# A second block with resident weights at one expert position, and an order table for the expert loads

## The reference

```python
def hierarchical_moe(x, wg, bg, we, be, w_gate, w_up, w_down):
    g_prob = softmax(xt @ wg + bg)            # 4 groups, the best one is taken
    e_top_l, e_idx = top_k(logits_of_the_8_experts_of_that_group, 2)
    gates = softmax(e_top_l) * g_top_p
    # each token goes to its 2 experts:
    hb = silu(xb @ w_gate[e]) * (xb @ w_up[e])      # 1024 -> 512
    y  = hb @ w_down[e]                             # 512 -> 1024, summed with the gates
```

## Time and profile before

| What | Value |
|---|---|
| Runs | 1364.5, 1366.34, 1366.96 us |
| Profiled execution: time / span | 1365.07 us / 1363.3 us |
| Mean granted TensorE clock | 0.876 |
| Busy share PE / DVE / ACT / POOL | 78% / 34% / 18% / 1% |
| Mean DMA rate over the span | 343 GB/s, 468.15 MB moved |
| Expert stage of layer 0, first streamed load issued / last down matrix landed | 163.57 us / 597.91 us |
| Expert stage of layer 1, the same | 898.37 us / 1347.15 us |

### The profile page before, as it was taken

The page is one execution under the profiler, slowest core; times in us unless marked ns, Lnnn a source line. Parts: engine busy times, 40 slices in busy tenths (PEclk is TensorE's granted clock), DMA queues, the critical chain, the costliest instruction groups (busy, mean ns, idle before and its releaser), DMA issues.

```text
span 1363.3 us, 21323 instructions
## 1 busy us (share of the span) xinstructions
PE 1069.8 (78%) x9301; PEld 717.3 (53%) x9301; DVE 464.2 (34%) x1167; ACT 244.5 (18%) x557; POOL 6.9 (1%) x28
## 2 busy tenths in 40 slices
PE   8999786856767686789999999887776585676775
PEld 7888543523434243447888888644434252343442
DVE  2351452222222122235655555463222222222123
ACT  2220111111111111123433333211111111111102
POOL 1000000000000000000000000000000000000000
PEclk9999888878877787889999999989788787887789
DMA  9754499999999999984566663469999999999995
GB/s 347 225 224 179 191 428 426 428 426 426 428 426 427 427 428 424 427 303 132 193 216 235 234 226 118 191 273 427 426 427 427 428 425 428 428 425 427 428 401 229
DMA packets 87941, 468.15 MB, mean 343 GB/s; under 512 B 16940, under 2 KB 56104, under 8 KB 62888
## 3 DMA queue, kind: packets, MB, share of 16 engines
q1 hardware_dynamic: 87344, 466.11, 84.2%
q10 hardware_dynamic: 504, 0.67, 0.2%
HBM read 465.68 MB, written 1.08 MB: 342 GB/s over the span
## 4 chain that ended last, share of the span: by engine, by line
PE 39%; issue 36%; DMA 22%; DVE 2%; SPq 1%; ACT 1%; POOL 0%; DVEq 0%; POOLq 0%
DMA w_gu<-in_expert_w_up 18%; PE pb L1192 10%; PE pa L1192 7%; PE acc L1216 4%; DMA w_x<-in_expert_w_up 3%; PE pa L1430 3%; PE wa L1430 2%; PE wb L1439 2%; PE acc L1318 2%; PE pb L1421 2%; PE pb L1247 1%; DMA w_dn<-in_expert_w_down 1%; PE pb L1408 1%; PE wa L1199 1%; PE wb L1619 1%
## 5 line engine op out<-in xcount | busy, mean ns | idle before, releaser
L1430 PE MATMUL pa<-w_gu,arena 128*32 128x256 f32 x1536 | 125.8, 499 | 81.5 <-DMA w_gu<-in_expert_w_up 81.5
L971 DVE TENSOR_SCALAR arena<-arena 128x128 f32<-128x128 f32 x64 | 14.5, 227 | 469.6 <-ACT arena L453 469.6
L1430 PE MATMUL wa<-w_gu,arena 128*32 128x256 f32 x1344 | 98.8, 459 | 64.0 <-DMA w_gu<-in_expert_w_up 62.4
L1430 PEld LDWEIGHTS pa<-w_gu,arena 128*32 128x32 f32 x1536 | 59.4, 142 | 153.0 <-DMA w_gu<-in_expert_w_up 93.7
L453 ACT ACTIVATE arena<-wb 32x256 f32<-32x256 f32 (+1 forms) x263 | 99.1, 377 | 134.7 <-PE wb L1439 122.7
L1192 PE MATMUL pb<-hnT,w_x 128*128 128x256 f32 x496 | 109.9, 380 | 2.4 <-DVE arena L1031 2.4
L1430 PEld LDWEIGHTS wa<-w_gu,arena 128*32 128x32 f32 x1344 | 48.6, 132 | 113.9 <-DMA w_gu<-in_expert_w_up 71.4
L1421 PE MATMUL pb<-arena,hs 128*128 128x128 f32 x480 | 79.5, 334 | 31.5 <-issue 15.1
L1192 PEld LDWEIGHTS pb<-hnT,w_x 128*128 128x128 f32 x496 | 93.4, 190 | 15.0 <-issue 2.8
L1421 PEld LDWEIGHTS pb<-arena,hs 128*128 128x128 f32 x480 | 73.2, 241 | 45.8 <-issue 41.4
L1439 PE MATMUL wb<-w_dn,arena 128*32 128x256 f32 x1440 | 89.2, 391 | 7.7 <-DMA w_dn<-in_expert_w_down 5.0
(11 more groups left out here) (285 smaller groups left out, 1196.1 us busy)
## 6 DMA issues: line engine op xcount, KB each, us to landing
w_dn<-in_expert_w_down SPq DMA_DIRECT2D x45, 2048.0 KB, 26.5
w_gu<-in_expert_w_gate SPq DMA_DIRECT2D x45, 2048.0 KB, 31.6
w_gu<-in_expert_w_up SPq DMA_DIRECT2D x45, 2048.0 KB, 36.0
arena<-in_expert_w_down SPq DMA_DIRECT2D x20, 2048.0 KB, 27.4
w_x<-in_expert_w_gate SPq DMA_DIRECT2D x20, 2048.0 KB, 31.2
w_x<-in_expert_w_up SPq DMA_DIRECT2D x20, 2048.0 KB, 35.7
w_x<-in_odd_in_proj SPq DMA_DIRECT2D x16, 1024.0 KB, 5.4
w_x<-in_odd_in_proj SPq DMA_DIRECT2D x16, 512.0 KB, 5.5
```

The source lines that it names most:

```text
L971: link(v.tensor_scalar(eg, eg, 1.0, None, ALU.add))
L1430: ins = mm(gu[32 * j:32 * j + 32, :, :], xb[:, k, c0:c0 + CAP], w_gu[s][:, :, k, P * j:P * j + P], start=(k == 0), stop=(k == KC - 1))
```

## The change

- `SLOT` is `e % 3` throughout, so the last four experts have the slots 1, 2, 0, 1.
- Position 15 (`WIDE`) has 64 slots. After its first 32 and the combine of its quad, all engines always run `second_block` on the weights that still lie in slot 0. This is in both layers, however many tokens there are.
- `swap_columns` on VectorE exchanges, in the routing tables, the first overfull expert with a number of at least 4 (`PRE`) and expert 15, and writes which expert stands at which position to `order`. SyncE reads each expert's number from `order` from position 4 on.
- The overflow loop is moved behind the second block, from position 27 to 15, and its loads use slot 0. SyncE asks for it before the load of position 18. Expert 15's first 64 tokens don't count as overflow.
- The token counts are taken in TensorE's `route`. `positions`, the copy `PG`, the first `rows_of` and `zero_acc` are moved from position 0 to position 1.
- Some semaphores are merged. The reserve columns of `pos` and their memset go.

The core of the diff:

```diff
-OV_AT = 28
-OV_SLOT = 1
-SLOT = [e % 3 for e in range(OV_AT)] + [2, 0, 1, 0]
+SLOT = [e % 3 for e in range(NE)]
+PRE = 4
+WIDE = 15
+OV_SLOT = SLOT[WIDE]
...
-            def expert_part(l, e, part, after=None):
+            def expert_part(l, e, part, after=None, which=None):
                 s = SLOT[e]
                 if after is not None:
                     sp_.wait_ge(S["dn_done" if part == 2 else "gu_done"], after + 1)
+                    if after % NE == WIDE:
+                        sp_.wait_ge(S["w_dn" if part == 2 else "w_gu"], after // NE + 1)
...
             def overflow_weights(l):
                 sp_.wait_ge(S["table_done"], l + 1)
-                sp_.wait_ge(S["gu_done"], NE * l + previous(OV_AT + 2) + 1)
-                sp_.wait_ge(S["dn_done"], NE * l + previous(OV_AT + 2) + 1)
+                sp_.wait_ge(S["w_dn"], l + 1)
                 k0 = sp_.value_load(table[0:1, l:l + 1], min_val=0, max_val=OV_LIST)
                 k1 = sp_.value_load(table[0:1, l + 1:l + 2], min_val=0, max_val=OV_LIST)
                 with sp_.If(k0 < k1):
...
+            def expert_at(l, e):
+                if e < PRE:
+                    return None
+                return sp_.value_load(order[0:1, NE * l + e:NE * l + e + 1], min_val=0, max_val=NE - 1)
+
             def expert_stream(l):
-                for e in range(3, NE):
-                    if e == OV_AT:
-                        overflow_weights(l)
-                    if e == OV_AT + 2:
+                for e in range(3, NE - 2):
+                    if e == PRE:
+                        sp_.wait_ge(S["order_done"], l + 1)
+                    which = expert_at(l, e)
+                    if e == WIDE + 3:
+                        overflow_weights(l)
                         k1 = sp_.value_load(table[0:1, l + 1:l + 2], min_val=0, max_val=OV_LIST)
                         sp_.wait_ge(S["ov_done"], k1 + 1)
...
+            def swap_columns(l):                      # VectorE, behind gathered(0, l, 1)
...
+                dve.wait_ge(S["cnt_done"], l + 1)
+                link(v.tensor_copy(cnt, wb[:, 0:NE]))
...                                                    # 8 small ones: prefer
+                link(v.tensor_reduce(out=most, in_=prefer, axis=AX, op=ALU.max))
+                link(v.tensor_scalar(other, prefer, most, None, ALU.is_equal))
...                                                    # 3 small ones: here, keep
+                link(v.tensor_tensor(cols2, cols, over(other), ALU.mult))
+                link(v.tensor_reduce(out=at_other[:, 0:6], in_=cols2, axis=AX, op=ALU.add))
...                                                    # 5 more over 6 x 32 columns
+                v.tensor_copy(order[0:1, NE * l:NE * l + NE], ids[0:1, :]).then_inc(S["order_done"], 1)
...
+            def second_block(l):                      # TensorE
+                pe.wait_ge(S["w_vec"], 3 * l + 1)
+                mm(o_B[:, :], o_sel, PG, start=True, stop=True)
+                for c in range(KC):
+                    for t in range(TT):
+                        ins = mm(o_XG[:, c, :], hs[:, t, c, :], o_S[:, t, :], start=(t == 0), stop=(t == TT - 1))
+                ins.then_inc(S["w_b"], 1)
+                pe.wait_ge(S["w_vec"], 3 * l + 2)
+                gate_up(o_xs, 0, SLOT[WIDE], GU[0]).then_inc(S["w_gu"], 1)
+                pe.wait_ge(S["w_vec"], 3 * l + 3)
+                down(o_hT, SLOT[WIDE]).then_inc(S["w_dn"], 1)
+                pe.wait_ge(S["w_act"], 2 * l + 2)
+                combine(l, o_G4, o_y).then_inc(S["w_done"], 1)
...
-                positions(l)
                 for e in range(NE):
...
-                    if e == 0:
+                    if e == 1:
+                        positions(l)
                         pe.wait_ge(S["pg_done"], l + 1)
-                    rows_of(e, l)
-                    if e == 0:
+                        rows_of(0, l)
                         zero_acc()
...
-                    if e == OV_AT - 1:
+                    if e == WIDE:
                         down_of(l, e)
                         combine_of(l, q)
                         pe.wait_ge(S["xs_done"], 2 * (NE // QUAD * l + q + 1) + 2)
+                        second_block(l)
```

More of the change, by code:

```diff
@@ L81 @@
 prep_sel quad_sel b_done g4_done gath_done xs_done gu_done gexp h_done ht_done dn_done y_copied comb_part
-ov_in ov_sel ov_b ov_x ov_gu ov_exp ov_ht ov_dn ov_yc ov_done
+order_done w_vec w_act w_b w_gu w_dn w_done
+ov_in ov_vec ov_act ov_b ov_gu ov_dn ov_done
 """.split()
@@ L148, in trunk_program @@
         ov_tot = sb("ov_tot", [P, 1])
-        ARENA = 11520
+        order = sb("order", [1, 2 * NE], I32)
+        slot_id2 = sb("slot_id2", [P, 1])
+        ARENA = 11392
         arena = sb("arena", [P, ARENA])
@@ L201, in trunk_program @@
         Rs = take(SEQ, rows=NG + NE + 1)
-        pos = take(TT, NE + QUAD)
-        gates = take(TT, NE)
+        cols = take(6, NE)
+        pos, gates, cnt, ids = cols[:, 0:TT, :], cols[:, TT:2 * TT, :], cols[:, 4, :], cols[:, 5, :]
+        other, here, keep, wide = (take(NE) for _ in range(4))
+        prefer, at_other, most = take(NE), take(8), take(1)
         mask = take(TT, NE)
         lg = take(TT, NG + NE)
-        rt1, rt2, oh1, oh2 = (take(TT, NE) for _ in range(4))
+        rts = take(4 * TT, NE)
+        rt1, rt2, oh1, oh2 = (rts[:, TT * i:TT * i + TT, :] for i in range(4))
+        cols2 = rts[:, 0:6, :]
         m8 = take(8, TT)
         dd, ee = take(TT, 8), take(TT, 8)
-        cnt = take(2 * NE + 8)
+        ov_more = take(NE)
         PG = take(2 * SEQ, rows=NE)
@@ L308, in overflow_weights @@
                         sp_.wait_ge(S["ov_done"], k + 1)
-                        e = sp_.value_load(table[0:1, ds(k + 3, 1)], min_val=0, max_val=NE - 1)
+                        p = sp_.value_load(table[0:1, ds(k + 3, 1)], min_val=0, max_val=NE - 1)
+                        e = sp_.value_load(order[0:1, ds(p + NE * l, 1)], min_val=0, max_val=NE - 1)
                         for part in range(2):
@@ L377, in _ @@
             expert_stream(0)
-            sp_.wait_ge(S["gu_done"], OV_AT + 1)
+            sp_.wait_ge(S["gu_done"], NE - 2)
             for c in (2, 1, 0):
@@ L932, in every_fourth, with second_select, second_block @@
                 return a.rearrange("p (m j) -> p j m", j=FF // P)
+            def second_select(l):
+                if l:
+                    dve.wait_ge(S["w_done"], l)
+                link(v.tensor_scalar(o_iota, iota1[:, :], float(CAP), None, ALU.add))
+                v.tensor_scalar(o_sel, ident[0:NE, WIDE:WIDE + 1].to_broadcast([NE, P]), 1.0, None, ALU.mult)
+                v.tensor_tensor(o_S, o_iota.unsqueeze(1).to_broadcast([P, TT, CAP]),
+                                pos[:, :, WIDE:WIDE + 1].to_broadcast([P, TT, CAP]), ALU.is_equal
+                                ).then_inc(S["w_vec"], 1)
+            def second_block(l):
+                dve.wait_ge(S["w_b"], l + 1)
+                link(v.tensor_scalar(o_G4, o_B[:, 0:SEQ], slot_id2[:, :], None, ALU.is_equal))
+                v.tensor_tensor(o_G4, o_G4, o_B[:, SEQ:], ALU.mult)
+                v.tensor_tensor(o_xs, o_XG, nffn[:, l, :].unsqueeze(2).to_broadcast([P, KC, CAP]), ALU.mult
+                                ).then_inc(S["w_vec"], 1)
+                dve.wait_ge(S["w_act"], 2 * l + 1)
+                link(v.tensor_scalar(o_eg, o_eg, 1.0, None, ALU.add))
+                link(v.reciprocal(o_eg, o_eg))
+                link(v.tensor_tensor(o_eg, o_eg, GU[0][:, 0, :], ALU.mult))
+                link(v.tensor_tensor(o_h, o_eg, GU[0][:, 1, :], ALU.mult))
+                v.transpose(out=o_hT, in_=every_fourth(o_h)).then_inc(S["w_vec"], 1)
             def overflow(k, l):
@@ L952, in overflow @@
                 oc.link(v.tensor_tensor(o_h, o_eg, GU[0][:, 1, :], ALU.mult))
-                v.transpose(out=o_hT, in_=every_fourth(o_h)).then_inc(S["ov_ht"], 1)
+                v.transpose(out=o_hT, in_=every_fourth(o_h)).then_inc(S["ov_vec"], 1)
                 assert oc.n == 9
@@ L1392, in route @@
                    ).then_inc(S["ranks"], 1)
+                mm(wb[:, 0:NE], ones[:, :], mask[:, 0, :], start=True, stop=False)
+                mm(wb[:, 0:NE], ones[:, :], mask[:, 1, :], start=False, stop=True).then_inc(S["cnt_done"], 1)
             def positions(l):
+                pe.wait_ge(S["order_done"], l + 1)
                 if l:
@@ L1400, in positions @@
                 ins.then_inc(S["pos_t"], 1)
-                mm(wb[:, 0:NE], ones[:, :], mask[:, 0, :], start=True, stop=False)
-                mm(wb[:, 0:NE], ones[:, :], mask[:, 1, :], start=False, stop=True).then_inc(S["cnt_done"], 1)
             def rows_of(e, l):
```

115 lines of the change are left out of this document (73 added, 42 removed).

## The result

The changed kernel takes 1376.27 us (median of 4 runs, 1375.48 to 1377.46). The kernel before took 1365.91 us beside it (4 runs, 1364.5 to 1366.96). The ratio is 1.0077, with a 95% interval of 1.006 to 1.0095: slower by 10.4 us, where 7.7 (from the profiled execution's own time) had been forecast. The profiled execution has a span of 1373.7 us and a time of 1375.48 us, at a mean granted clock of 0.876, as before.

The account below looks back on a forecast made before the run. Expert stages were taken as bound by the weight stream. 1365.07 - 15.4 - 2.0 + 15.0 + 10.1 = 1372.8 us, or 1374.0 with the median's step; predicted 1373.4, 8-in-10 range 1364 to 1380.

Parts of the forecast that it names:

- The reload of expert 29: Layer 1, positions 27 to 30: no second weight load, gain 15.4 us (three transfers 14.7, late issue 0.7).
- The early start: Start of each expert stage: `gate_up` of expert 0 overlaps the scaling without `positions` ahead, gain 1.0 us per layer.
- The swap: `swap_columns` on VectorE ahead of expert 0's activation: 5.3 us, hidden by the first two transfers, costing nothing.
- Layer 0's stall: Before position 18: load waits for `w_dn` (39.4 us behind position 15), 54.6 us instead of 44.5, 10.1 lost.
- The restart: Before position 18: 12.7 us from the load's issue on an idle queue to the landed up matrix.
- Layer 1's stall: Before position 18: load waits for `w_dn` (44.2 us behind position 15), 59.4 us instead of 44.4, 15.0 lost.
- The end: From the last `down` of layer 1 to the end of the span: no change, 0 us.
- The rival with the chain at 2.4 GHz: Second block at full clock: stalls 7.3 and 7.1 us, total 1362.1 us; chance 0.17 for full clock or most of it.
- Both blocks slow: Second blocks of both layers mostly at 1.2 GHz: stalls of 16 and 15 us, total 1378.7 us; chance 0.16.
- Loaded twice: Expert 29 still loaded twice: the 15.4 us not saved, a load behind each stall, 1388 us; chance 0.02.
- early loads dry: Stage start: `swap_columns` over 9 us delays the third transfer, some 2 us per layer, 1377; chance 0.05 including other delays.

Follow-up runs that it names:

- swap_late: Changed kernel with the body of `swap_columns` moved behind expert 0's activation, only the copy of the counts staying ahead: 1376.89 us, ratio 1.0065 to the kernel before.
- swap_twice: Changed kernel with the arithmetic of `swap_columns` run twice, 17 more instructions per layer ahead of expert 0's activation: 1386.07 us, ratio 1.0147 to the kernel before.
- after_again: The changed kernel measured once more, nothing altered: 1377.34 us, ratio 1.0085 to the kernel before.
- poll_late: Changed kernel with overflow poll and loop back at position 27; position 18's gate and up loads wait for the second `gate_up` alone: 1360.08 us, ratio 0.9944.
- no_reads: Changed kernel where SyncE, behind `w_dn`, reads nothing from `table` and has no overflow loop before position 18's loads: 1370.32 us, ratio 1.0023 to the kernel before.
- start_only: Kernel before with only the early start (token counts in `route`, `positions` and others moved to position 1), no swap or second block: 1365.64 us, ratio 0.999.
- block_l1: Changed kernel with the second block run in layer 1 only: 1364.73 us, ratio 0.9984 to the kernel before.
- ahead: Changed kernel with the second block's gather at position 14, its `gate_up` and `down` right behind position 15's: 1351.51 us, again 1350.31; ratios 0.9891, 0.9873.
- fixed_ids: Changed kernel with each position loading the expert of its own number, no reads of `order`: 1374.93 us, ratio 1.0057 to the kernel before.

## Why the prediction was right

Time, sign and mechanism came out as forecast. What was saved in bytes once was paid back as an empty queue twice. That the total is off by only 2.7 us is in part luck, since errors of both signs meet in it. By its steps:

- *The reload of expert 29.* Forecast -15.4, measured -14.5 by the stages. The three transfers were right; the 0.7 for the late issue was not there. Position 27 to 30 takes 45.0 us now (1290.92 to 1335.90).
- *The early start.* Forecast 1.0 us per layer. The gather's second half starts 2.68 us ahead of `gate_up(0)` in the earlier trace rows and 1.88 us ahead of it now, and the first load follows `gate_up(0)` after 3.72 us in both. In layer 0 it is 3.25 and 2.49. So 0.8 us per layer is what the rows show, the low bound. It is the overlap that was forecast: `gate_up(0)` starts at 904.12, at the gather's end, and VectorE scales the second half beside it. The other 0.2 us, half of it for the memset, is not to be seen.
- *The swap.* 5.2 us long and hidden, forecast 5.3 and hidden. `swap_late` shows that it costs nothing, and `swap_twice` that twice its length is no longer hidden.
- *Layer 0's stall.* Forecast 10.1, measured 10.9 to 13.8. `w_dn` at 39.1 us was forecast at 39.4 and the reads of 2.7 at 2.5. The restart took 13.8 us and not 12.7.
- *Layer 1's stall.* Forecast 15.0, measured 13.3. This is the term that was mis-sized: I took the block, from the end of the combine to `w_dn`, at 20.3 us from the earlier trace rows. It took 17.0 in both layers, near the 17.6 that I had taken for layer 0. The restart, again longer (13.5), added 0.8. The other profiles show that the choice itself was the wrong way round. In layer 1, which I had likened to position 27, the block takes 17.0 us in all eight profiles that have it. In layer 0 it takes 17.0 in three and 20.2 to 20.4 in four (`after_again`, `poll_late`, `no_reads`, `swap_late`). What decides between the two stays open.
- *The end.* Forecast nothing, measured +2.1. The last `down` and the last combine took 2.98 and 5.17 us, where the kernel before had:

```profile
1347.15 1.93 PE L1439 MATMUL wb<-w_dn,arena 128*32 128x256 f32 x32 [1.88 <-DMA w_dn<-in_expert_w_down]
...
1350.74 3.72 PE L1449 MATMUL acc<-arena 128*128 128x256 f32 x16 [1.65 <-ACT arena L453]
```

The granted clock there is 0.62 and 0.70 in the changed kernel, and was 1.00 before:

```profile
1355.00:1360.00 5.00, 2.98 (x32) 1.21 (x32) 0.00 (x0) 1.50 (x4) 0.00 (x0) 0.62 0.00 0
1360.00:1365.00 5.00, 4.96 (x16) 4.01 (x16) 1.99 (x3) 1.67 (x8) 0.00 (x0) 0.70 0.00 0
```

And the kernel before:

```profile
1347.00:1355.00 8.00, 5.66 (x48) 3.90 (x48) 2.57 (x4) 3.87 (x15) 0.00 (x0) 1.00 0.01 2
```

The second block has no part in this. `start_only` has none and took 3.10 and 6.72 us at this place, and `block_l1`, which has one, took 1.94 and 3.73. The granted clock stands at another level there from one profile to the next, and no run ties that to a part of the change. With the two stall errors (+0.8 and -1.7), the reload's (+0.9) and the start's (+0.6), it makes the 2.7 us that the sum was low.

*The rival with the chain at 2.4 GHz* gave 1362 us. It needed `w_dn` before 38 us. In the fifteen second blocks of the profiles (those of `ahead` aside) it came at 39.0 to 42.3 us, and the second `gate_up` took 4.94 to 6.56 us, never the 3.66 of the full clock. In layer 0 of the changed kernel the clock fell at 380, in the second block's gather, with TensorE busy for all of the 2.00 us before and behind it (the windows above). Even with the quad's gather at the full clock (`block_l1`) the stall is 10.6 us. Wherever the load waits for `w_dn` and the reads, the stall is 10.4 us or more; the rival's 7.3 and 7.1 us came in no profile of that kind. The Trainium skill, "TensorE: Matmul & The Clock Gate", section on the oscillation of the clock, has the clock fall after idle time. The windows at 378 and 380 disagree, as the earlier trace rows did; `swap_twice` agrees, where the clock fell while TensorE stood idle for 6.4 us.

*Both blocks slow* (1378.7) stands near by its number: the profiled execution of `after_again` took 1379.10 us. Its mechanism does not: there the stalls are 13.8 and 13.2 us and not 16 and 15, the block was slow in layer 0 alone, and its end took 3.8 us longer than that of the kernel before. *Loaded twice* is refuted by the 64 loads, *early loads dry* by `swap_late`.

*The restart.* From the issue to the start of the `gate_up` that waits it took 13.3 to 14.05 us, where the earlier trace rows had given 12.7. That was one row at the low end. The same view at the start of layer 0's stage in the kernel before, with two transfers issued on the idle queue as in the earlier trace rows:

```profile
w_gu<-in_expert_w_up SPq DMA_DIRECT2D x1, 2048.0 KB, 13.1
```

Over the profiles the up matrix landed 12.2 to 13.5 us after its issue at the starts of the stages, and 12.7 to 13.6 us where the queue had run empty behind position 15. In layer 0 the two kinds overlap (12.4 to 13.5, and 13.0 to 13.6), so most of what the forecast lacked there lies in having used a row of layer 1. In layer 1 they don't: 12.2 to 12.6, and 12.7 to 13.3. What stays open is this half a microsecond. Behind position 15 the down matrix follows the other two within a few microseconds, and at the start of a stage it does not; whether it takes bandwidth from them was not tried. The Trainium skill, "DMA: Bandwidth & Descriptors", section on the anatomy of one DMA, names a fixed 2.0 us, for transfers that GpSimd issues; those here are issued by SyncE. An estimate by it, with two matrices at 4.9, is 11.8 us; the rows are longer and decide.

## What to carry to other kernels

In a stage that is bound by a stream of loads, ask of added work not how long it is but which buffer it holds, and when that buffer's next load must be issued so that the queue doesn't run empty. The same second block costs 11 to 14 us per layer where it stands between `gate_up(15)` and the next load, and 0.6 us where it fills TensorE's waits for the stream. Put as few waits and register reads as the data need ahead of a load that is late, because there each of them lies on the path; where the queue is full, they cost nothing or next to it (`fixed_ids`).

## What the runs showed of the hardware

- The granted clock fell with TensorE busy without a break (from 0.99 to 0.50 at 380, in a gather of 32 matmuls of 32 columns), and it also fell with TensorE idle (`swap_twice`, at 171). The same chain of gather, `gate_up` and `down` of one kernel took 5.41 + 6.24 + 3.44 us in one execution and 4.96 + 5.03 + 1.93 in another. A term of a sum that is taken from one such row is uncertain by 3 us.
- From the semaphore to the issue, with two reads of a table value, a branch not taken, a third read and a wait between them, SyncE took 2.1 to 2.7 us. Without them it took 0.2.
- A stream that ran empty needed 13.3 to 14.05 us from the issue to the start of the `gate_up` that waits for two matrices of 2 MB; in the full stream the same two take 9.8. From issue to landing the second of the two took 12.2 to 13.6 us on an empty queue.
